# RG-LRU gate products of a hybrid encoder layer: from one 128-row block-diagonal product for each gate to one 64-row product for each head

## The chip, the cores and the metric

The kernel runs on one core of a Trainium2 chip. The metric is the device time of one execution in microseconds (us), smaller is better. A core has a matrix engine (TensorE, PE in the rows; its weight loads are PEld), VectorE (DVE), ScalarE (ACT), GpSimd (POOL) and SyncE (SP), which here only issues transfers. The engines run independent instruction streams, each in its own order, and meet at semaphores.

## What is computed

One layer runs over 2048 prompt tokens and 32 sample tokens. After a norm and an input product, 512 channels pass through a causal convolution of width 4 and the RG-LRU recurrence, 512 through a diagonal state-space recurrence (S5); a gated product, two norms, an output product and a SwiGLU feed-forward network of width 2816 follow. The change is in the two gates of the RG-LRU. They are block-diagonal: 8 heads of 64 channels, with a 64x64 matrix each for the recurrence gate (`wa`) and for the input gate (`wx`).

```python
xh = xf.reshape(B_, T, LRU_HEADS, LRU_HD)
r = jax.nn.sigmoid(jnp.einsum('bthi,hij->bthj', xh, wa).reshape(B_, T, W) + ba)
ig = jax.nn.sigmoid(jnp.einsum('bthi,hij->bthj', xh, wx).reshape(B_, T, W) + bx)
log_a = -LRU_C * r * jax.nn.softplus(-lam)
a = jnp.exp(log_a)
b = jnp.sqrt(-jnp.expm1(2.0 * log_a)) * (ig * xf)
```

## The kernel before

Channels lie on partitions and tokens along the free dimension. The 2080 tokens are cut into 5 blocks of T = 416; block 4 holds the last 384 prompt tokens and the 32 sample tokens. Everything up to the feed-forward network is called the mixer of a block. The mixer of block 0 runs first and alone, in the order of the list `FIRST`. From then on the feed-forward network of block b (22 pairs of `gate` and `up` products and the `dn` products behind each two pairs) is interleaved with the mixer of block b+1: the table `MIXER` gives for each mixer step the place among the 66 feed-forward steps behind which it stands. `STEPS` is the whole list, and every engine's code walks through it and emits its own part of each step, so the order on each engine is fixed when the program is built.

The 512 RG-LRU channels are 4 chunks (j = 0 to 3) of 128 partitions, which is two heads to a chunk: the even one on partitions 0 to 63, the odd one on 64 to 127. The steps that matter here:

- `cv` j: VectorE convolves a chunk into `tmp[:, 4 + j % 2]` (`conv`), and counts `conv_done`.
- `ga` j: TensorE makes two fp32 products of the convolved chunk (L859), one with the 128x128 matrix `w_gates[:, 0, j]` (both heads' `wa` on its diagonal) and one with `w_gates[:, 1, j]` (both `wx`). Each goes to a PSUM bank of its own. ScalarE reads each bank with one Sigmoid over 128 partitions (L714), into `tmp[:, 6 + j % 2]` and `tmp[:, j % 2]`, and frees the bank. In the program one such product is one instruction; in the trace each shows as two weight loads and two matmuls, so that a `ga` is a group of 4.
- `bx` j: VectorE multiplies the input gate with the convolved chunk. It first waits until the second bank of `ga` j has been read. `la`, `lb`, `lc`, `ld` make the decay, the root and the scan.
- `s5` j: TensorE makes the output product `y5` of pair j-2 (L869, L870) and the state product `v5` of pair j (L879). ScalarE reads `y5` with a Gelu (L732); VectorE reads `v5` (`s5prod`) and runs the scan.
- `dn`: 8 products into 3 banks, which VectorE adds to `x_acc` one by one.

The other mixer products, the gates, and `v5`, `y5` share three PSUM banks in a ring (banks 5 to 7, in the order of `USE`): `m_bank` makes TensorE wait until the use three before has been read. All the large products (L783 to L785) are three single fp32r products for one of fp32 precision: their weights are split into a high part by ScalarE (L606) and a low part by VectorE (L930, `w_hl`); L930 is the line of a helper through which nearly all of VectorE's products and sums go. SyncE loads the small arrays once at the start; `w_gates`, `carry5`, `conv_st` and `lru_st` count on the semaphore `par_c`, for which the first `cv` and every `ga` wait. Block 0 makes its input products in plain fp32 (L848), and sets up tables for S5 in between (L825 is a product with 16 weight columns).

Of the kernel before, what the change touches and what calls it, by code (L numbers as in the profile page):

```python
# [9 lines left out]
ACT = mybir.ActivationFunctionType  # L10

P = 128
# [8 lines left out]
NB, T = 5, 416  # L21
# [8 lines left out]
KL = LRU_W // P  # L30
G, HG, NP_ = 32, 16, 64
# [99 lines left out]
def build(nc, a, outs):  # L131

    with ExitStack() as ctx:
# [12 lines left out]
        def sb(name, shape, dt=F32):  # L146
            return at(name, shape, dt, take(4 * math.prod(shape[1:])))
# [1 line left out]

        ones = sb("ones", [P, P])  # L150
        ident = sb("ident", [P, P])
        w_gates = sb("w_gates", [P, 2, KL, P])
        vec = sb("vec", [P, 68])
        small = sb("small", [P, 20])
        carry5 = sb("carry5", [P, G, 2])
        conv_st = sb("conv_st", [P, KL, 2, CONV_W - 1])
        lru_st = sb("lru_st", [P, KL, 2])
# [9 lines left out]
        tmp = sb("tmp", [P, 8, T])  # L167
# [56 lines left out]
        acc = ctx.enter_context(nc.psum_tensor("acc", [P, 8, 512], F32))  # L224
# [10 lines left out]
        B_A, B_X, B_GLU, CONV, CONVB, LAM = 32, 36, 40, 44, 60, 64  # L235
        SGN, NS2PI, HPI, CL, NCL, N2CL = 0, 1, 2, 4, 8, 12

        def v1(c):
            return vec[:, c:c + 1]
# [5 lines left out]
        par_a, par_b, par_c, consts = sem("par_a"), sem("par_b"), sem("par_c"), sem("consts")  # L245
# [31 lines left out]
        def wait_m(eng, key):  # L277

            eng.wait_ge(m_full, USE[key] + 1)
            return SH + USE[key] % 3  # L280

        def m_freed(key):
            return m_free[USE[key] % 3]
# [36 lines left out]
        def _(sp):  # L320
# [31 lines left out]
            sp.dma_start(lmask[:], a["lmask"][:, 0:W5]).then_inc(par_b, 16)  # L352
            for u in range(2, RING):
                load_unit(u)
            for dst, name in ((w_gates[:], "w_gates"), (carry5[:], "carry5"), (conv_st[:], "conv_st"), (lru_st[:], "lru_st")):
                sp.dma_start(dst, a[name]).then_inc(par_c, 16)

            def load_v(gt):
# [15 lines left out]
            for step in STEPS:  # L374
                kind, b, j = step
# [218 lines left out]
        def _(act):  # L594
# [32 lines left out]
            for step in STEPS:  # L627
                kind, b, j = step
# [61 lines left out]
                elif kind == "us":  # L690
                    if b and j == 0:
                        act.wait_ge(nrm_lo, 2 * KL * b)
                    bank = wait_m(act, step)
                    act.activation(natural(zs[:, j]), tokens(acc[:, bank, 0:T]), ACT.Copy).then_inc(m_freed(step), 1)
                elif kind == "xl":
                    if b or j:
                        act.wait_ge(conv_done, b * KL + j)
                    bank = wait_m(act, step)
# [5 lines left out]
                elif kind == "gl":  # L704
                    if b and j == 0:
                        act.wait_ge(nrm_lo, 2 * KL * b)
                    bank = wait_m(act, step)
                    act.activation(y_lru[:, j, :], acc[:, bank, 0:T], ACT.Gelu_apprx_tanh).then_inc(m_freed(step), 1)
                elif kind == "ga":
                    if j >= 2:  # L710
                        act.wait_ge(ylru_done, b * KL + j - 1)
                    for g, (slot, bias) in enumerate(((6, B_A), (0, B_X))):
                        bank = wait_m(act, (*step, g))
                        act.activation(tmp[:, slot + j % 2, :], acc[:, bank, 0:T], ACT.Sigmoid, bias=v1(bias + j))\  # L714
                           .then_inc(m_freed((*step, g)), 1)
                elif kind == "la":
                    act.wait_ge(pl_done, 1)
                    for n in (2 * j, 2 * j + 1):
# [10 lines left out]
                elif kind == "s5" and j >= 2:  # L729
                    o = j - 2  # L730
                    bank = wait_m(act, ("y5", b, o))
# [14 lines left out]
                elif kind == "glu":  # L746
                    for g, n in enumerate((2 * j, 2 * j + 1)):
                        bank = wait_m(act, (*step, g))
# [22 lines left out]
                elif kind == "gate":  # L771
                    c = chunk(b, j)
# [8 lines left out]
        def _(pe):  # L781
# [5 lines left out]
            def m_bank(key):  # L787
                n = USE[key]
                if n >= 3:
                    pe.wait_ge(m_free[n % 3], n // 3)  # L790
                return SH + n % 3
# [22 lines left out]
            for step in STEPS:  # L814
                kind, b, j = step
# [4 lines left out]
                if kind == "ck":  # L820
                    pe.wait_ge(c1_done, j + 1)
                    for half in range(2):
                        bank = prep_bank(("ck", j, half))
# [4 lines left out]
                elif kind == "bt":  # L828
                    pe.wait_ge(bm_done, j + 1)
                    for half in range(2):  # L830
                        bank = prep_bank(("bt", j, half))
# [20 lines left out]
                        ready = (lambda k: pe.wait_ge(h_lo, split_at("h1", b) + k + 1)) if j == 0 else None  # L852
                        product(acc[:, bank, 0:T], UNIT[step], 0, hidden_x(b), KD, ready).then_inc(m_full, 1)
                elif kind == "ga":
                    pe.wait_ge(par_c, 64)
                    pe.wait_ge(conv_done, b * KL + j + 1)
                    for g in range(2):
                        bank = m_bank((*step, g))
                        pe.matmul(acc[:, bank, 0:T], w_gates[:, g, j, :], tmp[:, 4 + j % 2, :], start=True, stop=True)\  # L859
                          .then_inc(m_full, 1)  # L860
                elif kind == "s5":
                    if j >= 2:
# [58 lines left out]
        def _(v):  # L921
# [188 lines left out]
            for step in STEPS:  # L1110
# [51 lines left out]
                    h_lo_split(kind, b, H_PARTS[j][-1])  # L1162
                elif kind == "cv":
                    if (b, j) == (0, 0):
                        v.wait_ge(par_c, 64)
                    if j >= 2:
                        v.wait_ge(ylru_done, b * KL + j - 1)
                    wait_evacuated(v, ("xl", b, j))
# [158 lines left out]
```

## Time and profile before

| | |
|---|---|
| median of 3 runs | 2335.99 us (2334.59 to 2338.13) |
| the profiled execution's own time | 2338.14 us |
| its span in the trace | 2336.3 us |
| TensorE busy | 2218.3 us, 95% of the span |
| VectorE busy | 1538.7 us, 66% |
| ScalarE busy | 1091.2 us, 47% |
| the four gate matmuls of a `ga` | 20 times, 80 matmuls in the trace |

The span is what the trace covers; the time has some 2 us around it. Busy TensorE time is counted from modelled ends of overlapping matmuls, so that the distance between two starts says more than a duration. From 284 us on, when the mixer of block 0 is over, TensorE is nearly always busy; before that the other engines set the pace.

### The profile page before, as it was taken

What the parts mean: (1) busy time and instruction counts of PE and PEld (TensorE: products, weight loads), DVE (VectorE), ACT (ScalarE), POOL (GpSimd) and SP (SyncE); (2) the same over time, 40 slices, a digit from 0 to 9 for tenths busy, and PEclk for the clock granted to TensorE, in tenths of its full rate; (3) what the DMA queues carried; (4) which work ended last, traced back from release to release, by engine and by line L of the source; (5) the groups of instructions that cost most, each with busy time, mean ns of one, the idle gap of its engine ahead of it and who ended that gap; (6) DMA issues with size and microseconds to landing.
All of it is one profiled execution on the core that took longest, in us unless ns stands there. A gap on an engine that the chain in (4) does not pass through costs nothing.

```text
span 2336.3 us, 30354 instructions
## 1 busy us (share of the span) xinstructions
PE 2218.3 (95%) x11650; PEld 2129.7 (91%) x11650; DVE 1538.7 (66%) x2581; ACT 1091.2 (47%) x1459; POOL 418.8 (18%) x483
## 2 busy tenths in 40 slices
PE   4886899999999999999999999999999999999996
PEld 2565799999999999999999999999999999999996
DVE  7576546587756656876666587756657875665544
ACT  3455334564634455654444654634455563432232
POOL 7622101024011101221020023111102321100001
PEclk9966899999999999999999999999999999999998
DMA  4852333545333545553353656334455653343331
GB/s 160 219 173 73 115 117 115 154 153 183 120 117 118 176 132 153 163 162 109 117 176 108 148 170 178 123 112 128 162 141 153 165 150 108 118 142 113 112 127 63
DMA packets 191120, 322.82 MB, mean 138 GB/s; under 512 B 82944, under 2 KB 121152, under 8 KB 190848
## 3 DMA queue, kind: packets, MB, share of 16 engines
q1 hardware_dynamic: 188608, 313.54, 44.3%
q0 software_dynamic: 2368, 7.34, 1.0%
q8 instruction: 93, 1.52, 0.3%
q14 instruction: 51, 0.42, 0.1%
HBM read 296.39 MB, written 26.53 MB: 138 GB/s over the span
## 4 chain that ended last, share of the span: by engine, by line
PE 86%; DVE 6%; POOL 3%; ACT 2%; issue 1%; DMA 1%; POOLq 0%; SPq 0%; DVEq 0%; ACTq 0%
PE acc L783 27%; PE acc L785 26%; PE acc L784 26%; PE acc L870 1%; PE acc L869 1%; PE acc L879 1%; PE acc L859 1%; POOL tmp L502 1%; DVE rstd L1049 1%; PE acc L841 1%; PE acc L848 1%; DVE w_hl L930 1%; DMA t_dram<-tq 0%; DVE bmt L930 0%; DVE act_hl L930 0%
## 5 line engine op out<-in xcount | busy, mean ns | idle before, releaser
L783 PE MATMUL acc<-act_hl,w_hl 128*128 128x416 f32 x2544 | 908.4, 357 | 15.9 <-DVE act_hl L930 15.6
L785 PE MATMUL acc<-act_hl,w_hl 128*128 128x416 f32 x2544 | 898.4, 353 | 0.0
L784 PE MATMUL acc<-act_hl,w_hl 128*128 128x416 f32 x2544 | 895.3, 352 | 0.0
L930 DVE TENSOR_TENSOR w_hl<-w_raw,w_hl 128x1024 fp32r<-128x1024 f32 x428 | 529.7, 1251 | 79.8 <-ACT w_hl L606 78.4
L783 PEld LDWEIGHTS acc<-act_hl,w_hl 128*128 128x128 f32 x2544 | 482.1, 190 | 28.2 <-DVE act_hl L930 12.8
L784 PEld LDWEIGHTS acc<-act_hl,w_hl 128*128 128x128 f32 x2544 | 482.3, 190 | 10.1 <-issue 5.2
L785 PEld LDWEIGHTS acc<-act_hl,w_hl 128*128 128x128 f32 x2544 | 481.8, 189 | 0.9
L606 ACT ACTIVATE w_hl<-w_raw 128x1024 fp32r<-128x1024 f32 x428 | 442.2, 1051 | 66.7 <-DMA w_raw<-in_w_ffn 37.8
L930 DVE TENSOR_TENSOR x_acc<-x_acc,acc 128x416 f32<-128x416 f32 x480 | 273.1, 586 | 213.4 <-PE acc L785 206.9
L502 POOL TENSOR_TENSOR tmp<-tmp 128x416 f32<-128x416 f32 x135 | 171.3, 1269 | 1118.5 <-ACT tmp L614 1110.0
L783 PE MATMUL acc<-ff_hl,w_hl 128*128 128x416 f32 x880 | 311.7, 354 | 14.0 <-DVE x_acc L930 12.0
L785 PE MATMUL acc<-ff_hl,w_hl 128*128 128x416 f32 x880 | 306.5, 348 | 0.0
L784 PE MATMUL acc<-ff_hl,w_hl 128*128 128x416 f32 x880 | 306.5, 348 | 0.0
L930 DVE TENSOR_TENSOR f_g<-f_g,acc 128x416 f32<-128x416 f32 x110 | 64.5, 587 | 271.9 <-PE acc L785 271.7
L527 POOL TENSOR_TENSOR s5p<-s5w,s5t 128x216 f32<-128x216 f32 x80 | 103.4, 1292 | 740.8 <-DVE s5w L1107 740.8
L776 ACT ACTIVATE f_g<-acc 128x416 f32<-128x416 f32 x110 | 56.9, 517 | 330.5 <-PE acc L785 330.2
L783 PEld LDWEIGHTS acc<-ff_hl,w_hl 128*128 128x128 f32 x880 | 165.2, 188 | 19.5 <-DVE x_acc L930 16.2
L784 PEld LDWEIGHTS acc<-ff_hl,w_hl 128*128 128x128 f32 x880 | 165.5, 188 | 0.9 <-issue 0.3
L785 PEld LDWEIGHTS acc<-ff_hl,w_hl 128*128 128x128 f32 x880 | 165.2, 188 | 0.5
L614 ACT ACTIVATE tmp<-x_acc 128x416 f32<-128x416 f32 x120 | 63.4, 547 | 173.7 <-DVE x_acc L930 109.9
L624 ACT ACTIVATE ff_hl<-f_g 128x416 fp32r<-128x416 f32 x110 | 60.0, 546 | 131.7 <-DVE f_g L930 131.7
L930 DVE TENSOR_TENSOR s5prod<-acc,s5t 64x104 f32<-64x104 f32 (+5 forms) x288 | 66.5, 244 | 45.3 <-issue 32.8
(159 smaller groups left out, 1912.5 us busy)
## 6 DMA issues: line engine op xcount, KB each, us to landing
w_raw<-in_w_ffn SPq DMA_DIRECT2D x330, 512.0 KB, 3.7
w_raw<-in_w_in SPq DMA_DIRECT2D x60, 512.0 KB, 3.3
w_raw<-in_w_out SPq DMA_DIRECT2D x40, 512.0 KB, 3.3
s5y<-y_dram SPq DMA_DIRECT2D x80, 256.0 KB, 4.2
s5t<-t_dram SPq DMA_DIRECT2D x64, 162.0 KB, 3.8
s5v<-v_dram SPq DMA_DIRECT2D x80, 128.0 KB, 3.9
x_acc<-in_x SPq DMA_DIRECT2D x4, 1664.0 KB, 8.0
out_y<-x_acc SPq DMA_DIRECT2D x8, 832.0 KB, 6.5
```

Source lines behind the costliest of these rows:

```text
L502: po.tensor_tensor(tmp[:, 2, :], tmp[:, 6, :] if m == 1 else tmp[:, 2, :], tmp[:, 6 + m % 2, :], ALU.add)\
L527: po.tensor_tensor(s5p[:, s], s5w[:, s], tab[:, 0:2], ALU.mult).then_inc(p_made, 1)
L606: act.activation(w_hl[u % RING][:, 0, :], w_raw[u % RING][:], ACT.Copy).then_inc(w_hi, 1)
L614: act.activation(tmp[:, 6 + k % 2, :], src, ACT.Square).then_inc(sq_done, 1)
L624: act.activation(ff_hl[:, c % 3, 0, :], f_g[:, c % 2, :], ACT.Copy).then_inc(ff_hi, 1)
L776: act.activation(f_g[:, c % 2, :], acc[:, GATE, 0:T], ACT.Silu).then_inc(gate_free, 1)
L783: pe.matmul(out, w(0), x(0), start=first, stop=False)
L784: pe.matmul(out, w(0), x(1), start=False, stop=False)
L785: return pe.matmul(out, w(1), x(0), start=False, stop=last)
L841: pe.matmul(acc[:, bank, 0:T], ones[:], tmp[:, 2, :], start=True, stop=True).then_inc(m_full, 1)
L848: ins = pe.matmul(acc[:, bank, 0:T], w_raw[UNIT[step] % RING][:, k * P:(k + 1) * P], rows[:, k, :], start=k == 0, stop=k == KD - 1)
L930: return v.tensor_tensor(out, x, y, op)
```

## The change

`w_gates` is laid out anew. Each head has its own 64 rows, and on them 128 columns: its `wa` and its `wx`. On partitions 0 to 63 (even head) `wa` has columns 0 to 63 and `wx` columns 64 to 127; on partitions 64 to 127 (odd head) it is the other way round. A `ga` then is two products of 64 rows, h = 0 on the upper half of the array and h = 1 on the lower half, each again into a bank of its own. The results lie differently: in bank h the recurrence gate of head h is on the head's own partitions and its input gate on the other 64. ScalarE reads each bank with two Sigmoids of 64 partitions; the second writes to the other half of the partitions and takes its bias from `b_swap`, a copy of the input gate's bias with the halves exchanged. TensorE now waits for both banks before the first product. The arrays are loaded with six transfers of 64 partitions in place of one, so that `par_c` counts to 144.

```diff
-        w_gates = sb("w_gates", [P, 2, KL, P])
+        w_gates = sb("w_gates", [P, KL, P])
+        b_swap = sb("b_swap", [P, KL])
...
-            for dst, name in ((w_gates[:], "w_gates"), (carry5[:], "carry5"), (conv_st[:], "conv_st"), (lru_st[:], "lru_st")):
+            for o in (0, NP_):
+                for g in range(2):
+                    c = (g * NP_ + o) % P
+                    sp.dma_start(w_gates[o:o + NP_, :, c:c + NP_], a["w_gates"][o:o + NP_, g, :, o:o + NP_]).then_inc(par_c, 16)
+                sp.dma_start(b_swap[NP_ - o:P - o, :], a["vec"][o:o + NP_, B_X:B_X + KL]).then_inc(par_c, 16)
+            for dst, name in ((carry5[:], "carry5"), (conv_st[:], "conv_st"), (lru_st[:], "lru_st")):
...
-                    for g, (slot, bias) in enumerate(((6, B_A), (0, B_X))):
-                        bank = wait_m(act, (*step, g))
-                        act.activation(tmp[:, slot + j % 2, :], acc[:, bank, 0:T], ACT.Sigmoid, bias=v1(bias + j))\
-                           .then_inc(m_freed((*step, g)), 1)
+                    for h in range(2):
+
+                        own, other = (slice(0, NP_), slice(NP_, P)) if h == 0 else (slice(NP_, P), slice(0, NP_))
+                        bank = wait_m(act, (*step, h))
+                        act.activation(tmp[own, 6 + j % 2, :], acc[own, bank, 0:T], ACT.Sigmoid, bias=vec[own, B_A + j:B_A + j + 1])
+                        act.activation(tmp[own, j % 2, :], acc[other, bank, 0:T], ACT.Sigmoid, bias=b_swap[other, j:j + 1])\
+                           .then_inc(m_freed((*step, h)), 1)
...
-                    pe.wait_ge(par_c, 64)
+                    pe.wait_ge(par_c, 144)
                     pe.wait_ge(conv_done, b * KL + j + 1)
-                    for g in range(2):
-                        bank = m_bank((*step, g))
-                        pe.matmul(acc[:, bank, 0:T], w_gates[:, g, j, :], tmp[:, 4 + j % 2, :], start=True, stop=True)\
+                    banks = [m_bank((*step, h)) for h in range(2)]
+                    for h in range(2):
+                        r = slice(h * NP_, (h + 1) * NP_)
+                        pe.matmul(acc[:, banks[h], 0:T], w_gates[r, j, :], tmp[r, 4 + j % 2, :], start=True, stop=True)\
                           .then_inc(m_full, 1)
```

TensorE's order at the third `ga` of block 1 (between an `s5` and a feed-forward product; the brackets name the semaphores waited for, `m_free` being the ring's banks), before:

```order
L869 MATMUL acc<-u_74,s5y_85 128x52 [waits m_free1,y_in0,p_done]
L870 MATMUL acc<-s5x,s5y_85 128x52
L869 MATMUL acc<-u_74,s5y_85 128x52
L870 MATMUL acc<-s5x,s5y_85 128x52
L879 MATMUL acc<-u_74,s5v_84 128x52 [waits m_free2,v_in2]
L879 MATMUL acc<-u_74,s5v_84 128x52
L859 MATMUL acc<-tmp,w_gates 128x416 [waits m_free0,conv_done,par_c]
L859 MATMUL acc<-tmp,w_gates 128x416 [waits m_free1]
L783 MATMUL acc<-act_hl_77,w_hl_60 128x416 [waits up_free,w_lo]
L784 MATMUL acc<-act_hl_77,w_hl_60 128x416
```

and now (the new L870 is the old L859, L880/L881/L890 the old L869/L870/L879, L793 to L795 the old L783 to L785):

```order
L880 MATMUL acc<-u_75,s5y_86 128x52 [waits m_free1,y_in0,p_done]
L881 MATMUL acc<-s5x,s5y_86 128x52
L880 MATMUL acc<-u_75,s5y_86 128x52
L881 MATMUL acc<-s5x,s5y_86 128x52
L890 MATMUL acc<-u_75,s5v_85 128x52 [waits m_free2,v_in2]
L890 MATMUL acc<-u_75,s5v_85 128x52
L870 MATMUL acc<-tmp,w_gates 128x416 [waits m_free0,m_free1,conv_done,par_c]
L870 MATMUL acc<-tmp,w_gates 128x416
L793 MATMUL acc<-act_hl_78,w_hl_61 128x416 [waits up_free,w_lo]
L794 MATMUL acc<-act_hl_78,w_hl_61 128x416
```

The instructions stand in the same order; the wait for the second bank, `m_free1`, has moved from the second gate product to the first.

ScalarE's order at the fourth `ga` of block 1 (L606/L613 is a weight's high part, L732/L742 the read of `y5`), before:

```order
L606 ACTIVATE w_hl_57<-w_raw_63 128x1024 [waits w_in0]
L714 ACTIVATE tmp<-acc,vec 128x416 [waits m_full,ylru_done]
L714 ACTIVATE tmp<-acc,vec 128x416 [waits m_full]
L732 ACT_TABLE_LOAD
L732 ACTIVATE u_74<-acc 128x104 [waits m_full]
L606 ACTIVATE w_hl_58<-w_raw_64 128x1024 [waits w_in1]
```

and now (the new L723 and L724 are the two Sigmoids of a bank):

```order
L723 ACTIVATE tmp<-acc,vec 64x416 [waits m_full]
L724 ACTIVATE tmp<-acc,b_swap 64x416
L613 ACTIVATE w_hl_58<-w_raw_64 128x1024 [waits w_in0]
L723 ACTIVATE tmp<-acc,vec 64x416 [waits m_full,ylru_done]
L724 ACTIVATE tmp<-acc,b_swap 64x416
L723 ACTIVATE tmp<-acc,vec 64x416 [waits m_full]
L724 ACTIVATE tmp<-acc,b_swap 64x416
L742 ACT_TABLE_LOAD
L742 ACTIVATE u_75<-acc 128x104 [waits m_full]
```

Two Sigmoids of 128 partitions have become four of 64, and a bank is free behind the second and the fourth of them. VectorE's order is unchanged: behind this `ga` stand the `bx` product (`tmp<-tmp`, which waits for the fourth Sigmoid, as it did for the second), then `s5prod` and the scan, a weight's low part, and the sums of `dn`.

## Rows read from the trace of the kernel before

**Rows 1.** Windows: us; busy us (instructions) of PE, PEld, DVE, ACT, POOL; clock; DMA.
```profile
0.00:284.00 284.00, 201.14 (x762) 148.86 (x762) 191.07 (x351) 120.44 (x178) 122.45 (x144) 0.83 0.50 150
...
718.00:1152.00 434.00, 430.13 (x2322) 421.77 (x2321) 294.95 (x477) 219.20 (x290) 69.87 (x75) 0.99 0.47 143
```

**Rows 2.** Groups of ScalarE by line: busy us, mean ns | idle us before.
```profile
L714 ACT ACTIVATE tmp<-acc,vec 128x416 f32<-128x416 f32 x40 | 22.7, 605 | 18.1 <-PE acc L859 17.8
...
L653 ACT ACTIVATE kj<-acc 16x512 f32<-16x512 f32 x8 | 4.7, 587 | 2.4 <-PE acc L825 2.4
L660 ACT ACTIVATE btT<-acc 128x512 f32<-128x512 f32 x8 | 4.6, 596 | 10.2 <-PE acc L833 10.0 <-issue 0.3
```

**Rows 3.** Timeline, TensorE and its loads, first `ga` of block 1: start, us.
```profile
434.46 1.56 PE L859 MATMUL acc<-tmp,w_gates 128*128 128x416 f32 x4
...
435.85 0.19 PEld L784 LDWEIGHTS acc<-act_hl,w_hl 128*128 128x128 f32 x1 [0.16 <-issue]
```

**Rows 4.** Timeline, DVE, block 1, behind `ga` 0.
```profile
438.51 0.59 DVE L930 TENSOR_TENSOR tmp<-tmp 128x416 f32<-128x416 f32 x1 [1.23 <-ACT tmp L714]
...
446.54 0.59 DVE L930 TENSOR_TENSOR f_g<-f_g,acc 128x416 f32<-128x416 f32 x1 [5.17 <-PE acc L785]
```

**Rows 5.** Timeline, third `ga` of block 1.
```profile
501.37 0.26 ACT L732 ACTIVATE u<-acc 128x104 f32<-128x104 f32 x1
...
501.68 0.30 PEld L859 LDWEIGHTS acc<-tmp,w_gates 128*128 128x128 f32 x2 [0.81 <-ACT u L732]
...
502.49 0.19 PEld L784 LDWEIGHTS acc<-act_hl,w_hl 128*128 128x128 f32 x1 [0.16 <-issue]
```

**Rows 6.** Timeline, fourth `ga` of block 1 and what follows it.
```profile
507.95 1.25 ACT L714 ACTIVATE tmp<-acc,vec 128x416 f32<-128x416 f32 x2 [2.96 <-PE acc L859]
...
509.23 0.59 DVE L930 TENSOR_TENSOR tmp<-tmp 128x416 f32<-128x416 f32 x1 [1.38 <-ACT tmp L714]
...
509.92 0.82 DVE L930 TENSOR_TENSOR s5prod<-acc,s5t 128x104 f32<-128x104 f32 x3
...
513.83 0.46 PE L783 MATMUL acc<-ff_hl,w_hl 128*128 128x416 f32 x1 [0.53 <-DVE x_acc L930]
```

**Rows 7.** Timeline, DVE, fourth `ga` of block 4.
```profile
1814.57 1.02 DVE L930 TENSOR_TENSOR s5prod<-acc,s5t 128x96 f32<-128x96 f32 x6 [0.45 <-PE acc L879]
```

**Rows 8.** Timeline, weight loads where the tile of the array changes, block 0.
```profile
72.93 0.64 PEld L825 LDWEIGHTS acc<-c1t,bb 128*16 128x16 f32 x6
73.79 0.30 PEld L848 LDWEIGHTS acc<-rows,w_raw 128*128 128x128 f32 x2 [0.21 <-issue]
...
84.37 0.19 PEld L848 LDWEIGHTS acc<-rows,w_raw 128*128 128x128 f32 x1 [0.16 <-issue]
85.16 0.87 PEld L825 LDWEIGHTS acc<-c1t,bb 128*16 128x16 f32 x9 [0.60 <-issue]
```

**Rows 9.** Timeline, first and second `ga` of block 0.
```profile
117.95 1.11 ACT L714 ACTIVATE tmp<-acc,vec 128x416 f32<-128x416 f32 x2
119.09 0.59 DVE L930 TENSOR_TENSOR tmp<-tmp 128x416 f32<-128x416 f32 x1 [6.19 <-ACT tmp L714]
...
122.52 3.11 PE L859 MATMUL acc<-tmp,w_gates 128*128 128x416 f32 x4 [5.10 <-issue]
...
124.29 0.61 ACT L714 ACTIVATE tmp<-acc,vec 128x416 f32<-128x416 f32 x1 [5.23 <-PE acc L859]
...
127.01 7.94 PE L848 MATMUL acc<-rows,w_raw 128*128 128x416 f32 x16
```

**Rows 10.** Chain that ended last, block 0 at the fourth `ga`: start, us.
```profile
163.50 1.11 ACT tmp L714 x2
...
172.08 0.27 ACT u L732
```

**Rows 11.** SyncE's issue of the gate weights, and the first `cv` in the chain.
```profile
9.43 2.26 SPq L356 DMA_DIRECT2D w_gates<-in_w_gates  x1
...
97.28 0.89 DVE xl L1169
```

More of the change, by code:

```diff
@@ L1164, in _ @@
                     if (b, j) == (0, 0):
-                        v.wait_ge(par_c, 64)
+                        v.wait_ge(par_c, 144)
                     if j >= 2:
```

## The prediction

> **What bounds the kernel now.** I read the windows first, split where the mixer of block 0 ends. In a steady window of 434 us TensorE is busy for 430.13 us at full clock; in the first 284 us it is busy for 201.14 us, with a granted clock of 0.83 on average [rows 1]. So up to 284 us the chain between the engines sets the pace, and behind that TensorE's own stream does, except where it waits for a bank. The change has to be costed in both places, and in the steady one by where each of the four `ga` of a block stands.
>
> The timeline of a steady `ga` gives TensorE's price. The four matmuls begin at 434.46, and the next product's first matmul begins with the load of its second, at 435.85: 1.39 us for two products, so 0.35 us for each of the four matmuls [rows 3]. ScalarE's Sigmoid takes 0.605 us alone, and two behind each other 1.11 us, so 0.555 us each [rows 2, 9].
>
> **TensorE's part.** The product count stays, so the gain can come only from the two halves running side by side. Call the time of a `ga` T, now 1.40. No row shows a product on half the rows. Bounds: if the halves overlap wholly T is two matmuls, 0.70; if not at all, 1.40. The two matmuls of one product use the same rows and must follow each other, and the program has both of h = 0 ahead of both of h = 1. If TensorE starts them in that order, only the second of h = 0 and the first of h = 1 can lie side by side: three slots, 1.05.
>
> Then the array's tile changes. The nearest row is block 0's product with 16 weight columns between products of full width. The last full load starts at 84.37, its matmul with what would be the next load at 84.72, and the load of the narrow product could start then; it starts at 85.16, and the load of its successor shows a matmul starting 0.1 us behind the first load, so at 85.26 where 85.07 would be next: 0.2 lost. Going back, the last narrow load ends at 73.57 (72.93 + 0.64) and the full one starts at 73.79, idle 0.21: another 0.2 [rows 8]. So 0.4 for a pair of changes, if 64 rows count as 16 columns do; else 0. I take 1.05 + 0.4 = **T = 1.45**, the order in the program and the nearest row. The range is 0.70 to 1.80 (no overlap and 0.4).
>
> The Trainium skill bears on this in TensorEngine Tiling (Array Packing), Key Properties: a change of tiling mode, as opposed to a change of tile, drains the engine. Rows 8 agree for 16 columns; none shows it for 64 rows. By it alone the 0.4 stands; without it the sum below would be some 4 us smaller.
>
> **The four `ga` of a steady block.**
>
> - First and second: nothing waits, T - 1.40 = +0.05 each. ScalarE's two more Sigmoids (+1.11) delay VectorE's `bx`, which already waits for them until 438.51, but behind its next work VectorE sits idle for 5.17 us until TensorE's product ends at 446.54 [rows 4]. If that cover were gone, it would cost 1.11 each. Together **+0.1**.
> - Third: the second product waits for a bank that ScalarE frees with the Gelu of `y5`, 501.37 + 0.26. The load follows at 501.68, its matmul 0.1 later, and the next product starts at 502.49 [rows 5]. The first product used to run in front of this wait. Now both banks are waited for first: matmul at 501.78, plus T without the entry's 0.2 (TensorE is empty) gives 503.03, **+0.5**. With T = 0.70 it is 0.0.
> - Fourth: VectorE waits for the last Sigmoid, runs `bx` at 509.23, and goes straight on to `s5prod` at 509.92, the scan, a weight's low part and the sums of `dn`; TensorE waits for the first of those until 513.83, idle 0.53 [rows 6]. So VectorE is already late here, and what the Sigmoids add goes through undiminished. They start at 507.95 when the first bank is full; two ended at 509.20, four will end at 507.95 + 4 x 0.555 = 510.17: +0.97, and +0.2 more if the first product starts later by the entry. The time that TensorE saves or loses itself at this `ga` goes into this wait. `v5` behind it needs the first bank, free after two Sigmoids at 509.06, when TensorE comes to it anyway. **+1.2**.
>
> That is 1.8 us a block for blocks 1 to 3, 5.4. In block 4 VectorE waits for `v5` for 0.45 us ahead of `s5prod` [rows 7], which takes 0.4 off the 1.2: +1.4. Steady sum **+6.8**.
>
> **Block 0.** At the first `ga` the Sigmoids run from 117.95 to 119.06, VectorE has waited 6.19 us for them, convolves the next chunk only behind `bx`, and TensorE, idle for 5.10 us, starts the second `ga` at 122.52 [rows 9]: +1.11 for certain. The second starts at 123.63 then, at half clock. ScalarE began 1.77 us behind TensorE (124.29); so 125.40, four Sigmoids to 127.62, and the product behind the two `v5` needs the second gate bank: about 127.7, where it started at 127.01 [rows 9]. So of the 1.11 and the doubled Sigmoids together **+0.7** reaches the next product. At the third, `v5` gets its bank one Sigmoid later, but VectorE is busy convolving the last chunk: 0. At the fourth the Sigmoids at 163.50 (1.11 for two) are themselves in the chain that ended last, and from there it runs through ScalarE until 172.08 [rows 10]: **+1.1**. Sum +1.8.
>
> **Loads.** The weights were issued by 9.43 + 2.26 us, the first `cv` starts at 97.28 [rows 11]. Six smaller issues with short rows have 85 us to land, and SyncE has nothing behind them but loads that wait for products. 0; if the cover were gone, a few us once.
>
> **Sum.** 6.8 + 1.8 = +8.6. The profiled execution's own time is 2338.14, so 2346.7; the median of the three runs is 2.15 lower, so **2344.6 us**, 0.37% slower.
>
> **The rivals.** Each is the sum again with its own T.
> 1. Half rows are no change of mode: T = 1.05, no entry. First and second -0.35 each, third +0.35, fourth +0.97: +0.6 in three blocks, +0.2 in block 4, with block 0 +3.8: 2339.8. For it: the columns stay 128. Against it: the tile does change, as in [rows 8].
> 2. No overlap at all, and the changes cost: T = 1.80. +0.8, +0.85, +1.2, so 2.85 in three blocks and 2.4 in block 4, block 0 some 2.3 (half clock): +13.3, 2349.3. For it: in all the rows shown matmuls follow each other.
> 3. Not slower: the halves run wholly side by side, T = 0.70. -1.4, 0, +0.97, so -0.43 in three blocks, -0.85 in block 4, +1.8 in block 0: -0.4, 2335.6. It decides from T below 0.75. Against it: the order of the four matmuls.
> 4. The change does half of what it says for ScalarE: a Sigmoid of 64 partitions costs half. Then block 0 and the fourth `ga` cost next to nothing, and with T from 0.70 to 1.45 the sum is -6 to +3. Against it: 16 partitions x 512 take 0.587 us and 128 x 512 take 0.596 [rows 2], so time goes by the free size.
>
> On 3 the Trainium skill, TensorE: Matmul & The Clock Gate, Part 3, says that matmuls on different row groups start about 4 ns apart and span little over one. No row here shows that. As a mechanism of this kernel it is rival 3 if it holds for the whole products, three slots if it holds matmul by matmul in order.
>
> **How the numbers follow.** Forecast 0.42, rival 1 0.22, rival 2 0.13, rival 3 0.12, rival 4 0.04; 0.07 for what the shift does to the clock in block 0, in either direction. The measurement tells 0.2% (4.7 us) from no change. Faster needs rivals 3 or 4 and luck: 0.07. Same holds rival 1 and most of 3 and 4: 0.33. Slower: 0.60. The range leaves out the far end of rival 2 and what is faster than rival 3: 2335 to 2350; the forecast's own is 2341 to 2348.
>
> **What the profile after would show.** T: the start of the first matmul behind a steady first `ga`, 1.45 us behind the `ga`'s own. The third `ga` as one piece behind ScalarE's Gelu, with TensorE idle some 1 us ahead of it in place of between its products. Four Sigmoids of 64x416 at 0.6 us each; TensorE's wait for `x_acc` behind the fourth `ga` 1.5 to 1.7 us in place of 0.53. The second `ga` of block 0 about 1.1 us later. I am wrong if T is near 0.70, if the Sigmoids take half, or if the wait for `x_acc` does not grow.

## The result, and the profile after

The changed kernel takes 2347.36 us (median of 6 runs, 2343.43 to 2353.92), the kernel before 2337.06 us (median of 6, 2334.31 to 2340.23). The ratio is 1.0044, 95% interval 1.0031 to 1.0056: slower by about 10 us (7 to 13). The profiled execution of the changed kernel took 2343.43 us, with a span of 2341.6.

The same two windows as in [rows 1], with the same columns, now read:

```profile
0.00:284.00 284.00, 195.63 (x757) 144.39 (x757) 189.09 (x347) 124.28 (x183) 122.22 (x144) 0.81 0.50 149
718.00:1152.00 434.00, 427.55 (x2315) 418.82 (x2314) 293.65 (x476) 223.62 (x297) 69.57 (x75) 0.99 0.47 143
```

In the steady window TensorE is busy 2.58 us less and ScalarE 4.42 us more. The kernel is slower although its busiest engine has less to do. ScalarE's groups by line show where the rest of its time comes from (busy us, mean ns | idle us before). Forty Sigmoids of 605 ns [rows 2] are eighty of 603 ns:

```profile
L724 ACT ACTIVATE tmp<-acc,b_swap 64x416 f32<-64x416 f32 x40 | 24.1, 603 | 0.5
L723 ACT ACTIVATE tmp<-acc,vec 64x416 f32<-64x416 f32 x40 | 24.1, 603 | 9.2 <-PE acc L870 8.5
```

**The first `ga` of block 1**, which answers to [rows 3], in the timeline of TensorE and its loads (start, us):

```profile
436.82 0.30 PEld L870 LDWEIGHTS acc<-tmp,w_gates 64*128 64x128 f32 x4 [0.28 <-issue]
436.82 0.97 PE L870 MATMUL acc<-tmp,w_gates 64*128 64x416 f32 x4
...
437.72 0.19 PEld L793 LDWEIGHTS acc<-act_hl,w_hl 128*128 128x128 f32 x1 [0.60 <-issue]
...
437.83 0.19 PEld L794 LDWEIGHTS acc<-act_hl,w_hl 128*128 128x128 f32 x1
```

What to see here is "x4" in 0.30 us: four weight loads in one go, where before one load came per 0.35 us. The four matmuls, 0.97 us with the modelled end of the last one, take two slots in place of four. The loads sit idle for 0.28 us when they enter the 64-row tiles and for 0.60 us when they leave. I count as the prediction did. Without a change of tile the first matmul would have started at 436.73 (0.19 behind the 436.54 of the last product matmul), and the next product's second load starts at 437.83: T = 1.10 us. It is two slots of 0.35 and 0.4 for the pair of tile changes. Before it was 1.40.

**The third `ga` of block 1**, to be read with [rows 5]. TensorE's wait for ScalarE's Gelu has moved in front of both products:

```profile
503.10 0.26 ACT L742 ACTIVATE u<-acc 128x104 f32<-128x104 f32 x1
503.47 0.33 PEld L870 LDWEIGHTS acc<-tmp,w_gates 64*128 64x128 f32 x4 [1.09 <-issue]
503.50 0.97 PE L870 MATMUL acc<-tmp,w_gates 64*128 64x416 f32 x4 [0.99 <-ACT u L742]
...
504.51 0.19 PEld L794 LDWEIGHTS acc<-act_hl,w_hl 128*128 128x128 f32 x1
```

The Gelu ends at 503.36 and the product's second load follows 1.15 us behind. Before, 501.63 to 502.49 was 0.86 us [rows 5]. So this place costs 0.29 more.

**The fourth `ga` of block 1**, to be read with [rows 6]. ScalarE, VectorE and TensorE:

```profile
509.11 0.97 PE L870 MATMUL acc<-tmp,w_gates 64*128 64x416 f32 x4
...
510.17 0.60 ACT L723 ACTIVATE tmp<-acc,vec 64x416 f32<-64x416 f32 x1 [0.81 <-PE acc L870]
510.78 0.60 ACT L724 ACTIVATE tmp<-acc,b_swap 64x416 f32<-64x416 f32 x1
511.41 0.60 ACT L723 ACTIVATE tmp<-acc,vec 64x416 f32<-64x416 f32 x1
511.53 0.62 PE L890 MATMUL acc<-u,s5v 128*128 128x52 f32 x4 [0.43 <-ACT tmp L724]
512.03 0.60 ACT L724 ACTIVATE tmp<-acc,b_swap 64x416 f32<-64x416 f32 x1
512.66 0.59 DVE L941 TENSOR_TENSOR tmp<-tmp 128x416 f32<-128x416 f32 x1 [1.63 <-ACT tmp L724]
513.17 0.81 DVE L941 TENSOR_TENSOR s5prod<-acc,s5t 128x104 f32<-128x104 f32 x3
...
517.06 0.46 PE L793 MATMUL acc<-ff_hl,w_hl 128*128 128x416 f32 x1 [1.46 <-DVE x_acc L941]
```

The four Sigmoids start 0.61 to 0.63 us apart. `bx` follows the last of them, `s5prod` follows `bx`, and the wait of 0.53 us for `x_acc` is 1.46 us. A second wait is new, 0.43 us ahead of `v5` (L890). From the start of the `ga` to the product behind `x_acc` it is 7.95 us here. A later run of the kernel before (the last one below) has for the two:

```profile
509.34 1.56 PE L859 MATMUL acc<-tmp,w_gates 128*128 128x416 f32 x4
...
516.17 0.46 PE L783 MATMUL acc<-ff_hl,w_hl 128*128 128x416 f32 x1 [0.53 <-DVE x_acc L930]
```

That is 6.83 us, as in the first profile (507.00 to 513.83), so the fourth `ga` costs 1.12 more. Blocks 2 and 3 show 1.45 and 1.46 us for the wait. In block 4 it is 1.80, against 1.22 in that run of before, and the distance grows by 0.77.

**Block 0**, first `ga`, second `ga` and the projection behind it, which answers to [rows 9]:

```profile
113.43 0.97 PE L870 MATMUL acc<-tmp,w_gates 64*128 64x416 f32 x4
...
117.28 0.60 ACT L724 ACTIVATE tmp<-acc,b_swap 64x416 f32<-64x416 f32 x1
117.91 0.59 DVE L941 TENSOR_TENSOR tmp<-tmp 128x416 f32<-128x416 f32 x1 [9.08 <-ACT tmp L724]
121.35 1.76 PE L870 MATMUL acc<-tmp,w_gates 64*128 64x416 f32 x4 [6.95 <-DVE tmp L944]
...
125.71 1.03 PE L858 MATMUL acc<-rows,w_raw 128*128 128x416 f32 x1 [0.18 <-ACT tmp L724]
```

and TensorE's timeline at the third, with what waits for the Sigmoids:

```profile
152.97 0.97 PE L870 MATMUL acc<-tmp,w_gates 64*128 64x416 f32 x4
...
156.65 0.62 PE L890 MATMUL acc<-u,s5v 128*128 128x52 f32 x4 [1.22 <-ACT tmp L724]
157.88 0.64 PE L880 MATMUL acc<-u,s5y 128*128 128x52 f32 x2 [0.62 <-ACT tmp L724]
```

Before, the third `ga` began at 153.67, and the two products behind it read:

```profile
156.72 0.62 PE L879 MATMUL acc<-u,s5v 128*128 128x52 f32 x4 [0.57 <-ACT tmp L714]
158.17 0.42 PE L869 MATMUL acc<-u,s5y 128*128 128x52 f32 x2 [0.83 <-POOL carry L538]
```

`v5` waits for a gate bank for 1.22 us where it waited for 0.57, and starts 3.68 us behind the `ga` in place of 3.05. The next `s5` now waits for a bank too, 0.62 us, where it waited for GpSimd's `carry` for 0.83 before; it starts 4.91 us behind the `ga` in place of 4.50. Where the first `ga` of block 0 stands differs from profile to profile (112 to 118 us), so I measure from it to the first product of the feed-forward part, the one that waits for `act_hl`:

```profile
286.24 0.45 PE L793 MATMUL acc<-act_hl,w_hl 128*128 128x416 f32 x1 [0.92 <-DVE act_hl L941]
```

That is 172.81 us here and 168.15 us in the profile of before.

### The profile page after: what moved, and what is told of

Same layout as the page of the kernel before. It is cut to its first block, busy times and chain, and to the rows that moved or that the text cites. A ratio compares the mean times of both kernels' runs of the same rounds, so it can differ in the third digit from the quotient of the medians.

```text
span 2341.6 us, 30419 instructions
## 1 busy us (share of the span) xinstructions
PE 2209.1 (94%) x11650; PEld 2119.0 (90%) x11650; DVE 1539.5 (66%) x2581; ACT 1118.0 (48%) x1499; POOL 415.1 (18%) x483
## 4 chain that ended last, share of the span: by engine, by line
PE 88%; DVE 6%; ACT 3%; POOL 2%; issue 1%; DMA 0%; SPq 0%; POOLq 0%; DVEq 0%; ACTq 0%
PE acc L793 27%; PE acc L795 26%; PE acc L794 26%; PE acc L858 3%; PE acc L881 1%; PE acc L880 1%; POOL tmp L509 1%; PE acc L890 1%; DVE rstd L1060 1%; PE acc L851 1%; PE acc L870 1%; DVE w_hl L941 1%; DVE tmp L944 0%; DVE s5prod L941 0%; DVE act_hl L941 0%
## 5 line engine op out<-in xcount | busy, mean ns | idle before, releaser
L793 PE MATMUL acc<-act_hl,w_hl 128*128 128x416 f32 x2544 | 904.8, 356 | 18.2 <-DVE act_hl L941 17.9
L795 PE MATMUL acc<-act_hl,w_hl 128*128 128x416 f32 x2544 | 896.9, 353 | 0.0
L793 PEld LDWEIGHTS acc<-act_hl,w_hl 128*128 128x128 f32 x2544 | 481.1, 189 | 35.1 <-issue 17.1
L795 PEld LDWEIGHTS acc<-act_hl,w_hl 128*128 128x128 f32 x2544 | 480.8, 189 | 0.9
L613 ACT ACTIVATE w_hl<-w_raw 128x1024 fp32r<-128x1024 f32 x428 | 442.0, 1051 | 66.4 <-DMA w_raw<-in_w_ffn 36.7
L793 PE MATMUL acc<-ff_hl,w_hl 128*128 128x416 f32 x880 | 312.2, 355 | 17.4 <-DVE x_acc L941 15.4
L795 PE MATMUL acc<-ff_hl,w_hl 128*128 128x416 f32 x880 | 307.2, 349 | 0.0
L793 PEld LDWEIGHTS acc<-ff_hl,w_hl 128*128 128x128 f32 x880 | 165.8, 188 | 22.8 <-DVE x_acc L941 19.6
L795 PEld LDWEIGHTS acc<-ff_hl,w_hl 128*128 128x128 f32 x880 | 165.6, 188 | 0.5
```

The costliest lines, as they stand in the source:

```text
L613: act.activation(w_hl[u % RING][:, 0, :], w_raw[u % RING][:], ACT.Copy).then_inc(w_hi, 1)
L793: pe.matmul(out, w(0), x(0), start=first, stop=False)
L795: return pe.matmul(out, w(1), x(0), start=False, stop=last)
```

## The experiments

The theory, S: the loss is ScalarE's. Four Sigmoids in place of two let `bx` and two banks wait, at the fourth `ga` of each block and along block 0. What TensorE wins by its halves is small and goes into waits. The rival, T: the tile changes and the early wait for both banks cost TensorE the time, and the Sigmoids are hidden.

**The change again**, unaltered, as the yardstick of the others.

> The change unaltered, to see which of its differences come back. In the one trace of it the steady blocks gave 3 us (first and second ga -0.3 each, third +0.3, fourth +1.1 to +1.2 in three blocks, +0.8 in block 4) and block 0 some 5 us behind its first ga, against 4 us won ahead of it. If the 4 us ahead of the first ga are chance, a second trace has the first ga of block 0 anywhere between 113 and 117 us, and the steady numbers the same within 0.1 us. If the six small loads cause them, it is at 113 again. Time: 7 to 13 us over the kernel before.

Measured: 2346.16 us, ratio 1.0039 (1.0025 to 1.0053), span 2344.5. The waits for `x_acc` are 1.46, 1.46, 1.47 and 1.80 us, and block 0 takes 172.40 us by the distance above. All of it repeats. The first `ga` of block 0 stands at 112.47 us, but the six small loads are not shown to be the cause: over all profiles it is 112.13 to 118.03 with the six loads and 113.69 to 118.25 with the one.

**TensorE's part alone.** One Sigmoid over all 128 partitions for each bank:

```
-  act.activation(tmp[own, 6 + j % 2, :], acc[own, bank, 0:T], Sigmoid, bias=vec[own, ...])
-  act.activation(tmp[own, j % 2, :], acc[other, bank, 0:T], Sigmoid, bias=b_swap[other, ...])
+  act.activation(tmp[:, (6, 0)[h] + j % 2, :], acc[:, bank, 0:T], Sigmoid, bias=v1(...))
```

> TensorE as in the change (two products of 64 rows), but ScalarE reads each bank with one Sigmoid over 128 partitions, as before; so half of the gate values land on the wrong partitions and its outputs are not the reference's. Theory S (the loss is ScalarE's four Sigmoids, which VectorE and two banks wait for): the wait for x_acc behind the fourth ga falls back to 0.5 to 0.7 us, block 0 loses its 1 to 3 us, and what is left is 4 x (-0.3 -0.3 +0.3 +0.2): within 1 us of the kernel before, ratio 0.999 to 1.001. Theory T (the loss is TensorE's, from changing the tile of the array): the ratio stays at 1.003 to 1.005.

Measured: 2333.86 us, ratio 0.9996 (0.9988 to 1.0005). The first steady `ga` is that of the changed kernel, 0.97 us for the four. Behind the fourth `ga`:

```profile
510.92 0.46 PE L792 MATMUL acc<-ff_hl,w_hl 128*128 128x416 f32 x1 [0.69 <-DVE x_acc L940]
```

0.69 us is near the 0.53 of before, and block 0 takes 169.33 us. TensorE's part alone neither costs nor gives anything that can be measured (the interval allows 1 us lost to 3 us won). Theory T falls.

**ScalarE's part alone.** TensorE and the loads as before, each bank read by two Sigmoids of 64 partitions:

```
-  act.activation(tmp[:, slot + j % 2, :], acc[:, bank, 0:T], Sigmoid, bias=v1(bias + j))
+  act.activation(tmp[0:64, ...], acc[0:64, bank, 0:T], Sigmoid, bias=vec[0:64, ...])
+  act.activation(tmp[64:128, ...], acc[64:128, bank, 0:T], Sigmoid, bias=vec[64:128, ...])
```

> TensorE and the loads as before (two products of 128 rows), but ScalarE reads each bank with two Sigmoids of 64 partitions, both onto their own partitions; outputs as the reference's. Theory S: fourth ga +1.2 us in three blocks and +0.8 in block 4, third 0, block 0 +2 to +5: 6 to 10 us slower, ratio 1.003 to 1.004. Theory T: ratio 1.000 to 1.001. If the Sigmoids again start 0.62 us apart (0.51 between two of 128), the pace comes from the change of partitions and not from the crossing to the other half or from b_swap.

Measured: 2343.09 us, ratio 1.0032 (1.002 to 1.0044). The wait behind the fourth `ga` is that of the changed kernel, and block 0 takes 172.98 us:

```profile
517.52 0.46 PE L784 MATMUL acc<-ff_hl,w_hl 128*128 128x416 f32 x1 [1.44 <-DVE x_acc L931]
```

So the loss appears with the Sigmoids alone, at the same places. Theory S stands.

**Both products on one half.** Does the gain in T come from the halves, and what do the tile changes cost without it? The edit is `r = slice(0, 64)` for both products, which computes other gates than the reference.

> The change with both products on the upper half of the array, so that they cannot run side by side; the second product reads the upper half's data twice and the outputs are not the reference's. If the ga's 1.10 us in the trace is full overlap (0.70) plus 0.4 for two changes of the tile, a ga now takes 1.40 + 0.4 = 1.8 us. If it is three slots (1.05) and nearly no cost of the change, it takes 1.40 to 1.45.

Measured: 2355.15 us in a single run. The weight loads of the first `ga` of block 1, with the product's behind them:

```profile
436.97 0.29 PEld L870 LDWEIGHTS acc<-tmp,w_gates 64*128 64x128 f32 x2 [0.28 <-issue]
...
437.43 0.19 PEld L870 LDWEIGHTS acc<-tmp,w_gates 64*128 64x128 f32 x1 [0.16 <-issue]
437.77 0.19 PEld L870 LDWEIGHTS acc<-tmp,w_gates 64*128 64x128 f32 x1 [0.16 <-issue]
...
438.67 0.19 PEld L794 LDWEIGHTS acc<-act_hl,w_hl 128*128 128x128 f32 x1
```

Behind the first two, the loads come one by one again, 0.36 and 0.34 us apart. The last matmul before them started at 436.69, so without a change of tile the first would have started at 436.88, and T = 438.67 - 436.88 = 1.79: four slots and the same 0.4. So the two products overlap because they lie on different halves, and the tile changes cost 0.4 either way.

**Taking `bx` out of the way.** If the wait for `x_acc` is `bx` in front of `s5prod`, moving `bx` one place behind `s5` removes it. The same move in the kernel before is the control.

```
-  (37, ('ga', 3)), (37, ('bx', 3)), (37, ('s5', 5)), (38, ('la', 1))
+  (37, ('ga', 3)), (37, ('s5', 5)), (38, ('bx', 3)), (38, ('la', 1))
```

> The change, with the fourth bx step moved one place back, behind the first half of dn, so that on VectorE s5prod, the scan, the weight's low part and the first four sums no longer stand behind the product that waits for the fourth Sigmoid. If that wait is what the change costs at the fourth ga of the steady blocks, s5prod starts as soon as v5 is there (v5 waits for the second Sigmoid only): some 1.0 us earlier, TensorE's wait for x_acc falls from 1.46 to about 0.5 us, and the time by about 3.5 to 4 us against the change: ratio to the kernel before 1.002 to 1.003 in place of 1.004. If the wait for the bank is the one that decides, x_acc is as late as in the change and the ratio stays at 1.004.

> The kernel before with the same move. There v5 is full at about 509.8 us, when bx ends anyway, so nothing is won: x_acc wait 0.45 to 0.55 us, ratio 0.999 to 1.001. It would be under 0.999 if VectorE's order alone were worth something, and then the gain of the first run would not speak of the change.

Measured: with the change 2345.82 us, ratio 1.0034 (1.0021 to 1.0047); the kernel before with the move 2342.03 us, ratio 1.0016 (1.0007 to 1.0025). In the change the wait goes from 1.46 to that of before:

```profile
520.76 0.46 PE L793 MATMUL acc<-ff_hl,w_hl 128*128 128x416 f32 x1 [0.54 <-DVE x_acc L941]
```

The fourth `ga` takes 7.03 us by the distance above in place of 7.95. The control missed what I expected: the move costs the kernel before some 3.7 us, although its fourth `ga` takes the same 6.83 us with it (510.69 to 517.52). From the product behind `x_acc` to the projections of the next part it loses 0.25 us in block 1 (34.78 for 34.53); where the rest goes I did not find. So the wait for `x_acc` at the fourth `ga` is `bx`, shown, but this move is no repair, and whether the time falls by it is open: 1.0034 lies within the interval of the change itself. Set against its own control, the change with the move is slower by 0.0018, about 4 us (the two intervals, 0.0013 and 0.0009 to either side, just part them), and its block 0 is 3.4 us longer than the control's (172.83 and 169.44).

**The banks.** The second bank's wait put back in front of the second product:

```
-  banks = [m_bank((*step, h)) for h in range(2)]
   for h in range(2):
-      pe.matmul(acc[:, banks[h], 0:T], ...)
+      pe.matmul(acc[:, m_bank((*step, h)), 0:T], ...)
```

> The change, with the wait for the second bank back ahead of the second product. At the third ga the upper half's product can then run in front of the wait for ScalarE's Gelu, but the two products no longer run side by side there: after the Gelu one product of 0.70 is left, in place of two in 0.70. If the overlap is full, the next product starts at the same time as in the change, 1.15 us behind the Gelu's end, or up to 0.1 earlier; nothing is won by it. If it starts 0.3 us earlier, the early wait cost what the third ga lost (0.29 us).

Measured: 2349.86 us in a single run, which says nothing by itself. The third `ga` of block 1:

```profile
507.35 1.93 PE L869 MATMUL acc<-tmp,w_gates 64*128 64x416 f32 x4
...
508.01 0.26 ACT L742 ACTIVATE u<-acc 128x104 f32<-128x104 f32 x1
508.32 0.29 PEld L869 LDWEIGHTS acc<-tmp,w_gates 64*128 64x128 f32 x2 [0.68 <-ACT u L742]
...
509.32 0.19 PEld L794 LDWEIGHTS acc<-act_hl,w_hl 128*128 128x128 f32 x1
```

Gelu's end at 508.27 to the product's second load is 1.05 us, against 1.15 with the early wait and 0.86 before. Only 0.10 of the 0.29 was the early wait. The other 0.2 is leaving the 64-row tiles. The product that stands behind the bank's wait takes its full two slots, with its partner beside it or without.

**The order of the four Sigmoids.** A kernel with a single Sigmoid of partitions 0 to 63 for each bank, meant to price two that follow each other on the same partitions, gave no result. This one does: in the kernel before, partitions 0 to 63 of both banks first ("the lower half" in the next text), then 64 to 127 of both:

```
+  for part in (slice(0, 64), slice(64, 128)):
+      for g, (slot, bias) in enumerate(((6, B_A), (0, B_X))):
+          act.activation(tmp[part, ...], acc[part, bank, 0:T], Sigmoid, bias=vec[part, ...])
```

> The kernel before, with four Sigmoids of 64 partitions for each ga in another order: the lower half of both banks first, then the upper half of both. Between the first and the second, and the third and the fourth, the partitions stay the same. If the 0.62 us from start to start in e3 and in the change comes from going from one half of the partitions to the other, these pairs start 0.51 us apart and only the second and third 0.62; if it belongs to 64 partitions, all start 0.62 apart. The first bank is now free behind the third Sigmoid and not behind the second, so v5 behind the fourth ga starts some 0.6 us later than in e3, but bx ends later still; x_acc is waited for 1.2 to 1.5 us, and the ratio is again 1.002 to 1.004.

Measured: 2345.71 us, ratio 1.0043 (1.0029 to 1.0056). ScalarE at the third `ga`, each Sigmoid by itself:

```profile
509.76 0.60 ACT L715 ACTIVATE tmp<-acc,vec 64x416 f32<-64x416 f32 x1
...
510.27 0.59 ACT L715 ACTIVATE tmp<-acc,vec 64x416 f32<-64x416 f32 x1
...
510.87 0.60 ACT L715 ACTIVATE tmp<-acc,vec 64x416 f32<-64x416 f32 x1
...
511.38 0.59 ACT L715 ACTIVATE tmp<-acc,vec 64x416 f32<-64x416 f32 x1
```

Two on the same half start 0.51 us apart, as two of 128 partitions do in the kernel with TensorE's part alone (505.38 and 505.89). Where the half changes it is 0.60, and with a change of half at every step, as with ScalarE's part alone, 0.61 to 0.63 (510.63, 511.24, 511.87 and 512.48 at its fourth `ga`). The order saves 0.25 us of ScalarE's time, and no time of the kernel. The banks are freed only by the third and the fourth Sigmoid, and `v5`, at the fourth `ga`, needs the one that the third frees:

```profile
516.78 0.62 PE L881 MATMUL acc<-u,s5v 128*128 128x52 f32 x4 [0.57 <-ACT tmp L715]
...
521.56 0.46 PE L785 MATMUL acc<-ff_hl,w_hl 128*128 128x416 f32 x1 [0.69 <-DVE x_acc L932]
```

The wait for `x_acc` shrinks from 1.44 to 0.69, a wait of 0.57 ahead of `v5` takes its place, and the fourth `ga` takes 7.74 us by the distance above, 0.91 more than before. Block 0 takes 174.48 us.

**The kernel before again**, a single run.

> The kernel before, unaltered, for a second trace of block 0. If block 0 behind its first ga is steady from run to run, the fourth ga's end and the first feed-forward product are 168 to 169.5 us behind the first ga, as in the kernel before and in the two others with two Sigmoids (168.2, 169.3, 169.4), against 172.4 to 173.0 with four. If it is 171 or more, block 0's part in the loss is not shown.

Measured: 2337.15 us, span 2335.4. Block 0 takes 169.43 us, and the waits for `x_acc` are 0.53, 0.52, 0.53 and 1.22 us. With it the distance of block 0 has these values: with two Sigmoids 168.15, 169.33 (TensorE's part alone), 169.43 and 169.44 (the kernel before with `bx` late); with four 172.40, 172.81, 172.83 (the change with `bx` late), 172.98 (ScalarE's part alone), 174.21 (both products on one half), 174.48 (the other order) and 174.50 (the second bank's wait late). The groups don't touch. For the change itself it is 172.6 on average against 168.8 for the kernel before, two profiles each: +3.8. The kept traces also say where. From the first `ga` to the second it is 7.92 and 7.93 us with the change and 6.66 twice before, +1.3; from the first to the fourth 47.16 and 46.95 against 44.55 and 44.99, +2.3; from the fourth to the feed-forward product the other +1.5.

## Why the prediction was right, and where its terms were not

The time was forecast at 2344.6 us within 2335 to 2350, slower; it is 2347.4. The main mechanism was right: the loss sits at the fourth `ga` and in block 0 and is ScalarE's doubled Sigmoids. TensorE's part was not, and the way to the number was only partly right, term by term.

- **T = 1.45, three slots and 0.4.** It measured 1.10. The 0.4 for the pair of tile changes, taken from a 16-column product, holds for 64 rows, with and without overlap (1.10 and 1.79). The step that failed is "If TensorE starts them in that order, only the second of h = 0 and the first of h = 1 can lie side by side". The order in the program does not keep the halves apart: all four loads go in 0.30 us and the products overlap wholly. This was rival 3's mechanism with the forecast's tile changes, a pair that I had not costed, although the prediction had both. What I cited from the Trainium skill, TensorE: Matmul & The Clock Gate, Part 3, agrees with the trace in that two whole fp32 products take little more than one, two slots of 0.35 us in place of four; the 4 ns between their starts no row here shows.
- **First and second `ga`, +0.05 each.** They measured some -0.29 each: T is 0.30 less, and from one to the next it is 5.63 us after and 5.90 before. VectorE's late `bx` was covered, as forecast.
- **Third, +0.5.** It measured +0.29, since T is smaller: 0.2 for leaving the tiles, 0.1 for the early wait.
- **Fourth, +1.2.** It measured +1.12 in block 1, and +0.77 for +0.8 in block 4 (1.2 less 0.4). Errors cancel in it. The Sigmoids last 2.46 us in place of 1.25 (+1.21, and not +0.97, since they lie 0.62 apart and not 0.555), they begin 1.06 us behind the `ga` in place of 0.96, and `s5prod` begins 0.51 behind `bx`, where it was 0.69. So VectorE did not go straight on before, as the prediction read it: `v5`, which `s5prod` reads, ran from 509.22 to 509.83, and 0.18 of the added time was covered by that. That `v5` gets its bank "when TensorE comes to it anyway" was wrong, it waits for 0.43 us, but here that time goes into the wait for `x_acc` behind it: with `bx` late the 0.43 stays, and only 0.20 of the 1.12 is left (7.03 for 6.83). The wait for `x_acc` itself, 1.46, came out just under the 1.5 to 1.7 that the prediction named.
- **Steady sum +6.8.** From the rows it is three times -0.58 + 0.29 + 1.12 = +0.83, and -0.58 + 0.29 + 0.77 = +0.48 in block 4: +3.0. Over the whole of block 1, first `ga` to the product behind `x_acc`, it is 80.24 us after (436.82 to 517.06) and 79.37 in the later profile of before (436.80 to 516.17): +0.87. From the first feed-forward product to the span's end, the first pair of profiles, which spend nearly the same time at the lower clock there (26.6 and 27.5 us), gives 2341.6 - 286.24 = 2055.4 after and 2336.3 - 284.01 = 2052.3 before: +3.1.
- **Block 0, +1.8.** It measured +3.8. The failed step is "At the third, `v5` gets its bank one Sigmoid later, but VectorE is busy convolving the last chunk: 0". TensorE waits there for the bank for 1.22 in place of 0.57 us, and what VectorE does in that time does not hide it: from the third `ga` to the fourth it is 7.62 us in place of 6.74, in part at the lower clock. The other terms were too small as well: the second `ga` comes 1.3 later and not 1.11, the projection behind it 1.13 later (12.28 us behind the first `ga` for 11.15) and not 0.7, and behind the fourth `ga` it is 1.5 and not 1.1. That all of it is ScalarE's, the kernels with one part of the change alone show (169.33 and 172.98).
- **Loads, 0.** The last of the six is issued by 17.5 us, none takes more than 11.7 us to land, and the first `cv` starts at 93.22.

So 6.8 + 1.8 = 8.6 was forecast, and the rows give 3.0 + 3.8 = 6.8. That the totals are so near is luck: T was 0.35 us too long at every `ga`, block 0 was priced at half of what it cost, and the two errors cancel in part.

The measured 10 (7 to 13) is some 3 more than the rows give, and the likely rest is TensorE's clock behind block 0, which neither sum holds; no run tests this. From the first feed-forward product to the end the two profiles of the change take 2055.4 and 2059.6 us, the two of the kernel before 2052.3 and 2049.0: 6.8 more on average. They spend 26.6 and 34.3 us there at the lower clock, against 27.5 and 20.4, and such a stretch costs about half its length (below). By that, as an estimate, 3.3 of the 6.8 is the clock and 3.5 is the rows' 3.0. With block 0's 3.8 this makes 10.6. The mean spans of the same profiles, 2343.05 and 2335.85, are only 7.2 apart because the first `ga` of block 0 happens to stand 3.4 us earlier in the two of the change (112.95 for 116.38), so that they do not bear out the 6.8 of the rows.

No kernel tried is faster than the kernel before. The one without the doubled Sigmoids equals it, and leaves half of the gates on the wrong partitions.

## What to carry to other kernels

Before an edit saves TensorE's time by other tiles, count the instructions by which the next engine reads the result: here one that reads half the partitions takes as long as a whole one (603 ns for 605), and the doubled readers keep the second bank, and what is queued behind it, for 2.46 us in place of 1.25. A gain on the busiest engine (2.58 us in 434) is worth nothing at the places where that engine waits for a bank or a slower engine next. Price such an edit place by place, at each wait that follows the edited step, and check the start-up part by itself: here one block of five carried more than half of the loss that the rows show (3.8 of 6.8 us).

## What the runs showed of the hardware

- Two fp32 products of 64 rows on the two halves of the array overlap wholly, though each is two matmuls and they are in the program one product after the other: 1.10 us for both with the tile changes, 1.79 on one half. The four loads take 0.30 us together; on one half the first two take 0.29 and the others follow 0.36 and 0.34 us apart.
- Going into 64-row tiles and back costs 0.4 us together at full clock (1.10 us for two slots, 1.79 for four). Leaving them is 0.2 of it (1.05 us from the Gelu's end with one product, 0.86 before). The loads show the two as idle times of 0.28 and 0.60 us.
- ScalarE's instructions of 0.60 us start 0.51 us apart when they stay on the same partitions, and 0.60 to 0.63 apart when the half changes. In the changed kernel the third of four reads the same half as the second and writes another, and it too starts 0.63 behind it.
- Behind block 0 the granted clock falls from 2.4 to 1.2 GHz for stretches of some 3.4 or 6.8 us, near 565, 1000, 1435, 1822, 1874 and 2315 us in one profile or another. Just before those looked at, TensorE had waits ahead of a `y5` product (L869 or L880): 0.17 and 0.34 us before the one at 565 and 0.72 before the one at 998 in the kernel before, 1.09 before the one at 1001 in the change. A stretch of 3.4 us costs 1.6: the same part of block 1's feed-forward takes 77.95 us with one (548.36 to 626.31, the kernel before) and 76.38 without (551.60 to 627.98, the change).
- Behind block 0 they sum to 27.5 us in one profile of the kernel before and 20.4 in the other, and to 26.6 and 34.3 in the two of the change, the end of the program counted in. Over whole runs the change spends more time at the lower clock: its 12 runs have a mean granted clock of 0.9718 (0.968 to 0.975), and the 43 runs of the kernel before that were made beside the experiments 0.9739 (0.971 to 0.976), which is some 10 us more at 1.2 GHz. Part of it lies in block 0 (0.81 and 0.82 for 0.83 and 0.83 in the first 284 us of the profiles); how the rest is spread, and why the change draws more such stretches, no run here tells.
